# Post-norm reciprocal root written to PSUM, and the mixer's output projection as split fp32r products

## What is computed

```python
def post(j, z, y, w):          # norm after a sub-layer, and the residual
    return (z + w * (1 + ada[:, j, 2]) * _rmsnorm(y, prm['g_post'][l, j])).astype(z.dtype)

# in the mixer, after the branches o_a, o_b, o_c
merged = (jax.nn.sigmoid(ga) * (o_a @ prm['w_hg_proj'][l])
          + jax.nn.sigmoid(gb) * (o_b @ prm['w_sb_proj'][l])
          + jax.nn.sigmoid(gc) * (o_c @ prm['w_ml_proj'][l]))
y = (merged @ prm['w_out'][l]).astype(h.dtype)

x = post(0, x, _swiglu(pre(0, x), ...), 0.5)
y, st = _mix(pre(1, x), l, prm, past)
x = post(1, x, y, 1.0)
x = post(2, x, _swiglu(pre(2, x), ...), 0.5)
```

## Time and profile before

| | |
|---|---|
| median of 3 runs | 1912.64 us (1905.34 to 1914.37) |
| the profiled execution | 1915.48 us |
| its span in the trace | 1913.4 us |
| mean granted clock of PE over the span | 0.967 |
| busy: PE, DVE, ACT, POOL | 93%, 54%, 41%, 4% |

### The profile page before, as it was taken

One profiled execution on the slowest core, in us unless ns is written; L12 is line 12 of the kernel. 1 busy time (PEld: TensorE's weight loads), 2 busy tenths in 40 slices (PEclk: granted clock), 3 DMA queues, 4 the chain that ended last, 5 costly groups with the idle time before them and its releaser, 6 DMA issues. The chain is left out here.

```text
span 1913.4 us, 33255 instructions
## 1 busy us (share of the span) xinstructions
PE 1777.3 (93%) x12776; PEld 1541.9 (81%) x12776; DVE 1038.4 (54%) x1867; ACT 776.6 (41%) x1413; POOL 82.6 (4%) x111
## 2 busy tenths in 40 slices
PE   5999989999999997999959989899999899979997
PEld 3888878877876786998859879688778667869997
DVE  3555454566567635654355543556665675266554
ACT  3554344344433204654344543443445221056552
POOL 0000010000000001000010000100000000010001
PEclk8999989999999998999979999899999999989998
DMA  8678635536348732556537786255453596325651
GB/s 322 255 300 316 230 129 201 197 147 239 145 156 304 263 110 98 185 197 260 228 131 286 270 306 241 103 227 189 146 224 139 192 331 222 125 96 175 233 222 53
DMA packets 85951, 391.90 MB, mean 205 GB/s; under 512 B 12472, under 2 KB 17856, under 8 KB 55488
## 3 DMA queue, kind: packets, MB, share of 16 engines
q1 hardware_dynamic: 72816, 368.24, 52.6%
q10 hardware_dynamic: 13008, 21.94, 3.2%
HBM read 377.32 MB, written 12.83 MB: 204 GB/s over the span
## 5 line engine op out<-in xcount | busy, mean ns | idle before, releaser
L1046 DVE TENSOR_TENSOR ring_parts<-ring,pages_parts 128x1024 fp32r<-128x1024 f32 (+1 forms) x272 | 314.4, 1192 | 204.1 <-ACT pages_parts L1626 204.0
L534 PE MATMUL ps<-arena_parts,pages_parts 128*128 128x264 f32 x1408 | 364.1, 293 | 27.4 <-DVE xn_parts L1114 21.4
L535 PE MATMUL ps<-xn_parts,pages_parts 128*128 128x264 f32 x1408 | 358.8, 289 | 0.0
L1626 ACT ACTIVATE pages_parts<-ring 128x1024 fp32r<-128x1024 f32 (+1 forms) x272 | 267.8, 1025 | 186.8 <-DMA ring<-in_w_ffn_in 77.5
L534 PEld LDWEIGHTS ps<-arena_parts,pages_parts 128*128 128x128 f32 x1408 | 272.6, 194 | 48.0 <-issue 47.4
L535 PEld LDWEIGHTS ps<-xn_parts,pages_parts 128*128 128x128 f32 x1408 | 271.7, 193 | 0.0
L495 PE MATMUL ps<-xn,ring 128*128 128x264 f32 x896 | 212.6, 394 | 6.0 <-ACT xn L1633 6.0
L495 PEld LDWEIGHTS ps<-xn,ring 128*128 128x128 f32 x896 | 170.3, 193 | 39.8 <-issue 6.8
L539 PE MATMUL ps<-arena_parts,ring_parts 128*128 128x264 f32 x1408 | 197.0, 283 | 0.0
L534 PE MATMUL ps<-big_parts,pages_parts 128*128 128x264 f32 x704 | 177.7, 288 | 7.4 <-DVE gates_parts L1060 6.6
L539 PEld LDWEIGHTS ps<-arena_parts,ring_parts 128*128 128x128 f32 x1408 | 181.2, 188 | 0.0
(11 more groups left out here) (334 smaller groups left out, 2586.7 us busy)
## 6 DMA issues: line engine op xcount, KB each, us to landing
ring<-in_w_ffn_in SPq DMA_DIRECT2D x88, 1024.0 KB, 5.0
ring<-in_w_ada SPq DMA_DIRECT2D x32, 1536.0 KB, 6.6
ring<-in_w_a SPq DMA_DIRECT2D x32, 1536.0 KB, 7.5
ring<-in_w_ffn_down SPq DMA_DIRECT2D x32, 1408.0 KB, 6.7
pages<-in_k_pages SPq DMA_DIRECT2D x128, 256.0 KB, 5.6
pages<-in_v_pages SPq DMA_DIRECT2D x128, 256.0 KB, 4.0
ring<-in_w_ada SPq DMA_DIRECT2D x24, 1024.0 KB, 7.4
ring<-in_w_proj SPq DMA_DIRECT2D x8, 1536.0 KB, 9.4
```

The source lines that it names most:

```text
L534: mm(ps[:, b, 0:T], tile, hi[:, k, :], start=start, stop=False)
L535: return mm(ps[:, b, 0:T], tile, lo[:, k, :], start=False, stop=False)
L1046: v.tensor_tensor(ring_lo[:, r, at * P:(at + n) * P], w, whi[:, place, 0:n * P].bitcast(F32), ALU.subtract)\
L1626: A(whi[:, place, 0:n * P], ring[:, r, at * P:(at + n) * P], ACT.Copy).then_inc(S.whi_ready, 1)
```

## The change

Two edits. The root of the norm after a sub-layer is written by ACT's second step to `YRS`, 264 columns of PSUM bank 6, and `residual` reads it from there; the root of the norm before a sub-layer stays in `rs`. And the output projection uses `split_product`: DVE, once it has added the third branch of a chunk, also copies it rounded to `xhi` and subtracts, leaving the low part `mlo` in the memory of `merged`; PE starts once all 8 chunks are split. The splits of the four slots of `w_out` are put between the other work of ACT and DVE.

```diff
+        merged, mlo = big[:, 0:KC, :], big_parts[:, 0:KC, :]
+        YRS = ps[:, M2, 0:T]
...
                     r = open_slot(2)
                     for n in range(2):
-                        product(r, n * KC, lambda k: merged[:, k, :], KC)
+                        split_product(r, n * KC, xhi, mlo, KC)
...
-                    rss = rs[:, TP:T].unsqueeze(1).broadcast_to([P, KC, NB])
+                    rss = YRS[:, TP:T].unsqueeze(1).broadcast_to([P, KC, NB])
...
-                        v.scalar_tensor_tensor(residual_part(c), y[:, c, 0:TP], gtab[:, c, 0:1], rs[:, 0:TP],
+                        v.scalar_tensor_tensor(residual_part(c), y[:, c, 0:TP], gtab[:, c, 0:1], YRS[:, 0:TP],
...
+                ahead.follow(slots)
                 for s in range(4):
+                    ahead.take(6)
+                for s in range(4):
+                    if s == 3:
+                        split(2 * KC)
...
                             if br:
-                                ins_ = v.tensor_tensor(merged[:, c, :], merged[:, c, :], dst, ALU.add)
-                                if br == 2:
-                                    ins_.then_inc(S.mg, 1)
-                                    dve.wait_ge(S.mg, c + 1)
-                                else:
-                                    link(ins_)
+                                link(v.tensor_tensor(merged[:, c, :], merged[:, c, :], dst, ALU.add))
+                        link(v.tensor_copy(xhi[:, c, :], merged[:, c, :]))
+                        v.tensor_tensor(mlo[:, c, :], merged[:, c, :], xhi[:, c, :].bitcast(F32), ALU.subtract)\
+                            .then_inc(S.mg, 1)
                 clear_sum()
                 for s in range(4):
+                    if s < 3:
+                        split(2 * KC)
                     slots.take(2)
                     for n in range(2):
                         sum_squares()
...
-                def rsqrt(bank, width):
+                def rsqrt(bank, width, out=rs[:]):
...
-                    return A(rs[:], rs[:], ACT.Exp, scale=-0.5)
+                    return A(out, rs[:], ACT.Exp, scale=-0.5)
...
-                    rsqrt(Z, D).then_inc(S.yrs_ready, 1)
+                    rsqrt(Z, D, YRS).then_inc(S.yrs_ready, 1)
...
+                ahead.follow(slots)
+                split(2 * KC)
                 for s in range(4):
+                    if s < 3:
+                        split(2 * KC)
                     r, _, before = slots.take(2)
                     for n in range(2):
                         y_chunk(r, before + 2 + n, s * 2 + n)
```

More of the change, by code:

```diff
@@ L212, in build @@
         hid = big_parts[:, 0:FC, :]
-        merged = big[:, 0:KC, :]
+        merged, mlo = big[:, 0:KC, :], big_parts[:, 0:KC, :]
         gates, gate_parts = twins("gates", [P, 3 * KC, T])
@@ L1548, in _ @@
                 scale_table(2)
-                ahead.follow(slots)
                 split(2 * KC)
```

## The result

The changed kernel takes 1896.38 us (median of 18 runs, 1887.99 to 1913.42) against 1909.48 us before (18 runs, 1905.34 to 1914.37): ratio 0.9933, 95% interval 0.9918 to 0.9947. It was timed against the kernel before on three more occasions, as `e0_after`, `e7_after` and `e10_after`: 0.9893 (0.9869 to 0.9917), 0.9897 (0.9856 to 0.9937), 0.9893 (0.9868 to 0.9917). Over all 37 runs its median is 1893.7 us, over all 69 of the kernel before 1910.35 us: 16.7 us, where 13.9 were forecast. The first comparison alone gives 13.1 us, the three later ones 18.0, 20.2 and 20.3. The profiled execution took 1890.98 us with a span of 1888.7 us.

What follows compares the result with a forecast made beforehand. TensorE (PE), busy 93% of the span and holding 39% of the wait chain, was taken as the bound. Output projection 8.5 us plus residuals 5.4 us gave 13.9 us, from 1912.64 to 1898.7 us, range 1892 to 1906 us.

Steps and rivals of the forecast that it cites:

- The output projection, 5.0 us a layer: Output projection: a split product takes 2.93 us instead of 3.56, so 8 products save 5.0 us a layer.
- PE's longer wait, 0.78 us: Before the output projection: DVE's extra rounding copy and subtraction lengthen PE's wait by 0.78 us, to 1.84 us.
- The third rival: Start of output projection: PE's longer wait brings half clock for 4.4 us, half lost per layer; 1903.1 us, 8%.
- one wait of 1.97 us: Evidence against lost clock at the output projection: after this wait the earlier trace kept clock 1.00 over the whole stretch.
- POOL at 718 ns, 1.3 us a residual: Residuals: with the root in PSUM, POOL's adds take 718 ns instead of 902; with a shorter first multiply, 1.3 us each.
- The multiply: DVE's residual multiply: with one PSUM input, 425 ns against 477 for its first instance, saving 0.05 us.
- The surcharge for a PSUM source: Residual DVE instructions: the skill page's 120 fixed cycles against 58 would cost 0.13 us a residual, 0.8 us in total.
- ACT's exponential: Writing the root to PSUM: assumed 0.42 us, as to SBUF, with 0.06 us either way.
- How much of it arrives, 5.4 us of 7.8: Six residuals: 1.3 us at each third one, 0.4 or 1.0 at the others as PE runs at half clock; 5.4 us.
- the second rival: Residuals: PE's sums at half clock swallow the gain, leaving 3.4 us or less of 5.4; 1901 us, 14%.
- part two: Residuals: the root in PSUM stops DVE and POOL keeping each other waiting; 5.4 us over six residuals.
- The sum: Whole kernel: 8.5 us from the output projection plus 5.4 from the residuals, 13.9 us; median 1898.7 us, 0.73% faster.

Runs made afterwards that it cites:

- e0_after: The changed kernel, unaltered, timed again against the kernel before: 1893.26 us, ratio 0.9893.
- e7_after: The changed kernel, unaltered, timed once more on another occasion against the kernel before: 1892.18 us, ratio 0.9897.
- e10_after: The changed kernel, unaltered, timed on a further occasion against the kernel before: 1890.09 us, ratio 0.9893.
- e4_halves: The changed kernel, but each residual's multiply reads the root from PSUM for chunks 0 to 3 and from an SBUF copy for 4 to 7: 1900.71 us (one run).
- e1_root: The kernel before with only the root moved to PSUM, output projection still fp32: 1905.51 us, ratio 0.9968.
- e2_split: The changed kernel with the root back in SBUF, so the split output projection alone: 1902.91 us, ratio 0.9956 of the kernel before.
- e5_warm: The changed kernel with constant matmuls filling PE's pauses after post-norm and pre-norm sums around the inner residuals: 1892.24 us, ratio 0.9905 of the kernel before.

## Why the prediction was right, point by point

- **The output projection, 5.0 us a layer.** Right at full clock. A product takes 2.91 us for 2.93 forecast, no slot is late. From PE's first matmul to the post sum, layer 1 takes 1659.06 - 1634.27 = 24.79 us, against 732.25 - 702.27 = 29.98 us in layer 0 before: 5.2 us.
- **PE's longer wait, 0.78 us.** Right: 1.86 - 1.06 = 0.80 us.
- **The third rival, the wait costs the clock** (8%, 2.2 us a layer). Too low a chance: it happened at 9 of 14 places. Its price was lower, 1.5 us for the 2.2 assumed: from PE's first matmul to the post sum, layer 0 takes 717.03 - 690.70 = 26.33 us and layer 1, where the clock stayed, 24.79. In the four profiles of the changed kernel it happened at 4 of 8 places, so an execution gained some 2 x (5.2 - 0.8) - 1.5 = 7.3 us here, not 8.5. The step that failed took the earlier trace rows as evidence, one wait of 1.97 us in one execution, after which the clock stayed. The same program, with the same wait, goes both ways.
- **POOL at 718 ns, 1.3 us a residual.** Right in what it is worth (6.78 to 5.51 us), with adds of some 730 ns; the mechanism and, from `e4_halves`, its cause were right too. The multiply was mis-sized: 474 ns, not the 425 ns of the earlier trace rows and no shorter than the undisturbed 477 ns of the earlier trace rows; that was worth 0.05 us a residual. The surcharge for a PSUM source that the Trainium skill gives in "VectorE: DVE Perf Modes", section "The TRN2 errata", does not show in it: 474 ns with the root in PSUM, 477 with both tensors in SBUF. ACT's exponential takes 0.39 us into PSUM, for 0.42 assumed:

```profile
718.30 0.39 ACT L1609 ACTIVATE ps<-rs 128x264 f32<-128x264 f32 x1
```

- **How much of it arrives, 5.4 us of 7.8.** Too low. Layer 0 before its second FFN: 0.4 forecast, 1.2 in the first profile and 16.62 - (747.97 - 732.13) = 0.8 in `e7_after`. Read at all six places (post sum to the first matmul of the next stage, or to POOL's end in the third sub-layers), 1.3, 1.2, 1.3, 1.3, 1.2 and 1.3 us arrive in the first profile, 7.6 in all; 6.9 in `e0_after`, 6.4 in `e7_after` and 5.3 in `e10_after`, a mean of 6.5. The step that failed took half clock during the sums, from one profile, as fixed: PE at 0.89 us a tile could not have used POOL's pace. Where half clock does cover the sums, nothing arrives, as the second rival has it. The first residual of `e10_after`, PE:

```profile
263.08 0.71 PE L595 MATMUL ps<-wbuf,consts 128*128 128x264 f32 x2 [1.23 <-DVE wbuf L1070]
267.28 6.83 PE L590 MATMUL ps<-xn,consts 128*128 128x264 f32 x16 [3.49 <-ACT xn L1604]
277.11 3.33 PE L496 MATMUL ps<-xn,ring 128*128 128x264 f32 x7 [3.00 <-ACT xn L1638]
```

This is 277.11 - 263.08 = 14.03 us, as in the kernel before (14.01), against 12.71 at full clock. But how long half clock lasts differs from execution to execution, and mostly it ended earlier. So the mechanism was right and its frequency was not; for the whole of part two the rows speak against the second rival. `e1_root`, 5.8 us with an interval of 2.9 to 9.6, agrees, but would not exclude it alone.
- **The sum.** 13.9 us forecast; 13.1 in the first comparison, 16.7 over all runs. That the rows of the two stages come so near to it is in part luck: 7.3 + 6.5 = 13.8 us, a projection that gave less than its 8.5 and residuals that gave more than their 5.4. The other 3 us were not settled. PE's waits for a split piece of weights elsewhere (line 534, in the change 535, on DVE's subtraction), which the prediction did not count, sum over the execution to 6.7 us in the profile before and 5.6 in `e1_root`, but to 0.9 in `e2_split` and to 1.1, 4.0, 2.1 and 1.6 in the four profiles of the changed kernel. They may be part of the rest; why they shrink was not tested. Mean granted clock, where it was recorded, is 0.969 over 37 runs after and 0.966 over 51 before, which by the line in the last section would be some 4 us; where in the kernel it lies was not looked at.

## What to carry to other kernels

Where GpSimd works beside VectorE, look for VectorE instructions that read two SBUF tensors; moving one input to PSUM frees both engines, here 474 ns against up to 945 for the one and 0.68 us against 0.87 a chunk for the other. How much of it reaches the time depends on the engine that follows. A wait of TensorE that the rows put at 1 to 2 us should be priced with some half clock behind it at some odds (here 1.5 us at 9 of 14 places), and is best removed by letting the first product start on the first finished chunk. Half clock alone is no loss to be won back: price it only where no other engine is also late, since filling it with idle matmuls around the residuals gave nothing that the timing could show.

## What the runs showed of the hardware that I had not expected

The spread of this kernel goes with TensorE's clock. In the 18 runs of the first comparison, time falls with the mean granted clock along a line (correlation -0.95): 1888.0 us at 0.972, 1913.4 at 0.957, some 15 us for 0.01. The line is no price of the clock everywhere: `e5_warm` had 0.008 more and was no faster. In the two profiles compared here the loss lies in the mixer. One row each for the mixer of layer 0, from the end of the pre norm's sums to the post sum, in the first profile of the changed kernel and in `e7_after`:

```profile
273.60:717.00 443.40, 421.61 (x2765) 1.00 0.55 195
```
```profile
275.20:732.10 456.90, 436.55 (x2764) 0.96 0.53 189
```

The same program took 13.5 us longer there, as much as the whole change gives (the whole spans differ by 9.1 us). And the clock did not fall behind a long pause: in `e7_after` PE had waited a mere 0.22 us,

```profile
358.30 0.71 PE L828 MATMUL ps<-wbuf,consts 128*128 128x264 f32 x2 [0.22 <-ACT wbuf L1857]
```
```profile
357.00:359.00 2.00, 1.78 (x14) 1.00 0.00 0
359.00:361.00 2.00, 2.00 (x12) 0.54 0.00 0
361.00:363.00 2.00, 2.00 (x13) 0.61 0.05 12
```

with 16 matmuls of one column each from 355.74 us on, and the same behind 423.37 us, one head later. In the profile of the kernel before it fell behind the same two sums (0.50 from 361 to 363 us, 0.51 from 425 to 427), so this is no effect of the change. In the first profile of the changed kernel the clock stayed at this place. What sets it off was not tested.
